# Thirty-six units of the first context pass in rounded products, with the convolution's taps divided anew between GpSimd and VectorE

## The reference, cut to what matters

```python
hc = modulate(rmsnorm(xc, norm1_g[l]), csh1, csc1)      # 256 x 1024
pc = hc @ w_in[l]                                       # 1024 x 4608: 36 tiles of 128 columns
q_c, k_c, v_c = (split_heads(u) for u in jnp.split(pc[..., GLU_END:QKV_END], 3, axis=-1))
...
yc_conv = conv_branch(pc[..., :GLU_END], conv_dw[l], conv_dw_b[l], conv_ln_g[l],
                      conv_ln_b[l], w_conv_out[l])      # 31 taps, 512 channels
yc_attn = merge_heads(context_attention(q_c, k_c, v_c)) @ w_na_out[l]
xc = xc + cg1 * gated_merge(pc[..., QKV_END:], yc_conv, yc_attn, w_out[l])
```

```python
def conv_branch(p_glu, dw, dw_b, ln_g, ln_b, w_o):
    a, g = jnp.split(p_glu, 2, axis=-1)
    u = a * jax.nn.sigmoid(g)
    u = dwconv1d(u, dw, dw_b)
    u = jax.nn.silu(layernorm(u, ln_g, ln_b))
    return u @ w_o
```

## Time and profile before

| what | before |
|---|---|
| times of three executions | 2887.86, 2890.33, 2897.75 us; median 2890.33 us |
| profiled execution | 2888.0 us, span of its instructions 2885.9 us |
| mean granted clock of TensorE | 0.98 of full speed |
| TensorE busy | 2788.7 us, 97% of the span |
| GpSimd, VectorE, ScalarE busy | 1303.7, 1511.6 and 1083.6 us |

### The profile page before, as it was taken

The page is one execution under the profiler, slowest core; times in us unless marked ns, Lnnn a source line. Parts: engine busy times, 40 slices in busy tenths (PEclk is TensorE's granted clock), DMA queues, the critical chain, the costliest instruction groups (busy, mean ns, idle before and its releaser), DMA issues.

```text
span 2885.9 us, 41322 instructions
## 1 busy us (share of the span) xinstructions
PE 2788.7 (97%) x15778; PEld 2293.2 (79%) x15778; DVE 1511.6 (52%) x1960; ACT 1083.6 (38%) x1667; POOL 1303.7 (45%) x752
## 2 busy tenths in 40 slices
PE   8998887999999999999999999999999999999998
PEld 7975744878888878877788888888887778788887
DVE  7855687353323345368874532422454887552535
ACT  4435223333323223235543422322343554342433
POOL 3423323435444264278842322222347884344343
PEclk9989889999999999999999999999999999999999
DMA  5246297323232243432231212121233222232332
GB/s 190 92 169 248 89 276 240 104 94 103 84 106 88 92 128 127 151 99 88 70 93 61 73 59 70 62 66 59 65 104 112 94 66 88 80 102 95 95 102 73
DMA packets 109735, 306.88 MB, mean 106 GB/s; under 512 B 29008, under 2 KB 37328, under 8 KB 109072
## 3 DMA queue, kind: packets, MB, share of 16 engines
q1 hardware_dynamic: 87584, 284.49, 30.7%
q10 hardware_dynamic: 19648, 16.66, 1.9%
q0 software_dynamic: 2352, 3.67, 0.4%
HBM read 294.95 MB, written 7.45 MB: 105 GB/s over the span
## 4 chain that ended last, share of the span: by engine, by line
PE 87%; DVE 5%; issue 2%; POOL 2%; DVEq 1%; ACT 1%; DMA 1%; SPq 0%; ACTq 0%; POOLq 0%
PE ps L296 41%; PE ps L330 17%; PE ps L321 6%; PE ps L1953 3%; PE ps L1949 3%; PE ps L1954 3%; PE ps L1957 3%; PE ps L2366 2%; POOL wlo L257 2%; PE ps L2026 1%; PE ps L2007 1%; PE ps L741 1%; DVE nacc L443 1%; PE ps L1995 1%; PE ps L1997 1%
## 5 line engine op out<-in xcount | busy, mean ns | idle before, releaser
L257 POOL TENSOR_TENSOR wlo<-wraw,whi 128x1024 fp32r<-128x1024 f32 x373 | 923.7, 2487 | 1279.6 <-ACT whi L249 1277.2
L249 ACT ACTIVATE whi<-wraw 128x1024 fp32r<-128x1024 f32 x373 | 391.7, 1055 | 457.6 <-PE ps L296 169.9
L296 PE MATMUL ps<-xah,whi 128*128 128x512 f32 x992 | 387.9, 391 | 1.7 <-issue 1.7
L296 PE MATMUL ps<-xal,whi 128*128 128x512 f32 x992 | 387.4, 391 | 0.0
L296 PE MATMUL ps<-xah,wlo 128*128 128x512 f32 x992 | 280.1, 391 | 0.0
L2252 DVE SCALAR_TENSOR_TENSOR co<-ub,vec,co 128x512 f32<-128x512 f32 (+1 forms) x216 | 255.6, 1222 | 4.2
L296 PEld LDWEIGHTS ps<-xah,whi 128*128 128x128 f32 x992 | 186.1, 188 | 42.7 <-issue 2.7
L296 PEld LDWEIGHTS ps<-xal,whi 128*128 128x128 f32 x992 | 186.1, 188 | 40.3
L296 PEld LDWEIGHTS ps<-xah,wlo 128*128 128x128 f32 x992 | 186.1, 188 | 40.2
L2353 POOL TENSOR_TENSOR co<-co,ct 128x512 f32<-128x512 f32 (+1 forms) x144 | 165.4, 1148 | 20.5
L296 PE MATMUL ps<-hhi,whi 128*128 128x512 f32 x408 | 159.3, 390 | 0.0
(11 more groups left out here) (417 smaller groups left out, 6011.4 us busy)
## 6 DMA issues: line engine op xcount, KB each, us to landing
wraw<-stream SPq DMA_DIRECT2D x425, 512.0 KB, 3.5
wada<-w_ada SPq DMA_DIRECT2D x96, 512.0 KB, 6.7
biasb<-attn_bias ACTq DMA_DIRECT2D x32, 256.0 KB, 3.3
xin<-x0T SPq DMA_DIRECT2D x4, 528.0 KB, 6.4
s_u<-uk ACTq DMA_DIRECT2D x8, 264.0 KB, 2.5
res<-x0T ACTq DMA_DIRECT2D x1, 2048.0 KB, 11.1
outT<-res SPq DMA_DIRECT2D x4, 512.0 KB, 2.6
s_y<-yk POOLq DMA_DIRECT2D x56, 32.0 KB, 5.5
```

What stands on the lines that cost most here:

```text
L249: act.activation(whi[:, s], wraw[:, s], ACT.Copy).then_inc(hi_done[s], 1)
L257: pool.tensor_tensor(wlo[:, s], wraw[:, s], whi[:, s].bitcast(F32), ALU.subtract).then_inc(lo_done[s], 1)
L296: last = pe.matmul(ps[:, bank, 0:b - a], w[:, s, kt], x[:, kt, c0 + a:c0 + b], start=start, stop=stop)
```

## The change

Three things change in pass c0, and the later passes keep their code.

1. Units U to U+35 go the split way (36 units); only U+36 to U+51 stay whole (`N_WHOLE` = 16). So `norm_hi_act` writes `xah` and `norm_scale_dve` also writes `xal` for c0a (eight more VectorE instructions), ScalarE does 36 more `split_hi`, GpSimd 36 more `split_lo`. The `split_hi` of U to U+3 stand in `mlp_act` ahead of the squares m = 4 to 7.
2. GpSimd does taps 0 to 9 of its two tiles (`CTX_TAPS` = 10) and two `split_lo` ahead of each of its nine tap steps; VectorE does the other 21 taps of tiles 0 and 1 behind its own.
3. VectorE does `some(3)` in place of `some(2)` at the end of each stage.

```diff
+CTX_TAPS = 10
-N_WHOLE = 52
-N_UNITS = N_B1 + N_WHOLE + 2 * N_LAYER + 8
-WHOLE = (N_B1, N_B1 + N_WHOLE)
+N_CTX, N_WHOLE = 52, 16
+N_UNITS = N_B1 + N_CTX + 2 * N_LAYER + 8
+WHOLE = (N_B1 + N_CTX - N_WHOLE, N_B1 + N_CTX)
...
     def norm_scale_dve(...):
-            if not one:
-                b = shift(kt) if shift else 0.0
-                dve.scalar_tensor_tensor(ylo[:, kt, 0:T], t(kt), b, yhi[:, kt, 0:T].bitcast(F32),
-                                         ALU.add, ALU.subtract).then_inc(n_lo.sem, 1)
+            b = shift(kt) if shift else 0.0
+            dve.scalar_tensor_tensor(ylo[:, kt, 0:T], t(kt), b, yhi[:, kt, 0:T].bitcast(F32),
+                                     ALU.add, ALU.subtract).then_inc(n_lo.sem, 1)
...
     def mlp_act(act, context):
         for kt in range(NT):
-            norm_hi_act(act, first, kt, CTX, context.modv(0), one=True)
+            norm_hi_act(act, first, kt, CTX, context.modv(0))
         for m in range(NT):
+            if m >= R:
+                split_hi(act, N_B1 + m - R)
             norm_square(act, NORM["final1"], m, lambda kt: res[:, kt], SEQ,
...
     class Pass:
-            self.one = whole(U)
-            self.taps = KTAP if self.one else POOL_TAPS
+            self.one = key == "c0"
+            self.taps = CTX_TAPS if self.one else POOL_TAPS
...
     def pe_filler(pe, p, g):
-        (here if p.one else hi_split)(pe, g, 0, 0)
+        hi_split(pe, g, 0, 0)
...
-        if p.one:
-            for kt in range(NT):
-                last = pe.matmul(o, wraw[:, s, kt], x1[:, kt, 0:p.T], start=kt == 0, stop=kt == NT - 1)
-            last.then_inc(unit_done[s], 1)
-            return
...
     def mix_dve(dve, p):
             if n < p.N:
-                some(1 if p.lat else 2)
+                some(1 if p.lat else 3)
...
     def mix_pool(pool, p):
-        T, l = p.T, p.l
+        T, l, per = p.T, p.l, 2 if p.one else 1
...
         for k in range(1, p.taps):
-            if p.U + 11 + k < p.U + 40:
-                split_lo(pool, p.U + 11 + k)
+            for g in range(p.U + 12 + (k - 1) * per, p.U + 12 + k * per):
+                if g < p.U + 40:
+                    split_lo(pool, g)
...
-        for g in range(p.U + 11 + p.taps, p.U + 40):
+        for g in range(p.U + 12 + (p.taps - 1) * per, p.U + 40):
             split_lo(pool, g)
...
     @block.sync
-            segment(N_B1, N_B1, R)
-            segment(N_B1 + R, N_B1 + R, N_WHOLE - R)
+            segment(N_B1, N_B1, N_CTX - N_WHOLE)
+            segment(WHOLE[0], WHOLE[0], R)
+            segment(WHOLE[0] + R, WHOLE[0] + R, N_WHOLE - R)
...
     @block.gpsimd
-            pool_units(pool, U_GLU, (N_B1 - U_GLU) // R - 1)
+            pool_units(pool, U_GLU, (N_B1 - U_GLU) // R)
```

More of the change, by code:

```diff
@@ L443, in norm_add, with norm_act @@
             dve.tensor_tensor(a, a, nsq[:, kt % 2, 0:T], ALU.add).then_inc(n_acc.sem, 1)
-    def norm_act(act, n, T, eps, split=True, shift=None, dst=None, sums=6, one=False, between=None):
+    def norm_act(act, n, T, eps, split=True, shift=None, dst=None, sums=6, between=None):
         norm_root_act(act, n, T, eps, sums)
@@ L453, in norm_act @@
             for kt in range(NT):
-                norm_hi_act(act, n, kt, T, shift, dst, one)
+                norm_hi_act(act, n, kt, T, shift, dst)
     def root_ahead(act):
@@ L474, in scaled_tile, with norm_hi_act @@
         return ps[:, 4 + kt % 2, 0:T] if n in (NORM["l0a"], NORM["l1a"], NORM["l1b"]) else ntt[:, kt % 2, 0:T]
-    def norm_hi_act(act, n, kt, T, shift=None, dst=None, one=False):
+    def norm_hi_act(act, n, kt, T, shift=None, dst=None):
         act.wait_ge(n_t.sem, n_t.past("t", t_before[n] + kt))
         b = shift(kt) if shift else 0.0
-        act.activation((x1 if one else (dst or halves(T))[0])[:, kt, 0:T], scaled_tile(n, kt, T), ACT.Identity, bias=b).then_inc(n_hi.sem, 1)
+        act.activation((dst or halves(T))[0][:, kt, 0:T], scaled_tile(n, kt, T), ACT.Identity, bias=b).then_inc(n_hi.sem, 1)
     def raw_hi_act(act, n, kt, src, g, dst):
@@ L530, in norm_rows_pe, with norm_dve @@
         last.then_inc(n_row.sem, 1)
-    def norm_dve(dve, n, src, T, gain, split=True, shift=None, dst=None, one=False):
+    def norm_dve(dve, n, src, T, gain, split=True, shift=None, dst=None):
         norm_rec_dve(dve, n, T)
         if split:
-            norm_scale_dve(dve, n, src, T, gain, shift, dst, one)
+            norm_scale_dve(dve, n, src, T, gain, shift, dst)
         else:
@@ L562, in norm_in_place_dve, with norm_scale_dve @@
         dve.drain()
-    def norm_scale_dve(dve, n, src, T, gain, shift=None, dst=None, one=False, also=None):
+    def norm_scale_dve(dve, n, src, T, gain, shift=None, dst=None, also=None):
         r = norm_row_dve(dve, n, T)
@@ L598, in build @@
         done += 0 if "final" in name else NT
-        kept_lo += 0 if "final" in name or name == "c0a" else NT
+        kept_lo += 0 if "final" in name else NT
     g1 = lambda name: (lambda kt: colr(name, 1, kt))
@@ L1755, in mlp_dve @@
             add_unit_dve(dve, N_B1 - 8 + m, 0, 0, m, res, SEQ)
-        norm_scale_dve(dve, first, context.src, CTX, context.gain(0), context.modv(0), one=True)
+        norm_scale_dve(dve, first, context.src, CTX, context.gain(0), context.modv(0))
         for m in range(R, NT):
@@ L1801, in build @@
     shared = {}
-    U_KV = N_B1 + N_WHOLE + N_LAYER
+    U_KV = N_B1 + N_CTX + N_LAYER
     class Pass:
@@ L2030, in whole_of @@
     def whole_of(p, x):
-        return {id(xah): x1, id(hhi): h1, id(mhi): m1}[id(x)] if p.one else x
+        return {id(hhi): h1, id(mhi): m1}[id(x)] if p.one else x
     def mix_pe(pe, p):
-        xh = whole_of(p, xah)
         if p.one:
-            pe_quad(pe, p.U, 0, 0, xh, xal, p.T, between=lambda: norm_sums_pe(pe, NORM["final1"], SEQ), **normed(p.key + "a"))
+            pe_quad(pe, p.U, 0, 0, xah, xal, p.T, between=lambda: norm_sums_pe(pe, NORM["final1"], SEQ), **normed(p.key + "a"))
             norm_rows_pe(pe, NORM["final1"], SEQ)
@@ L2723, in ffn_dve @@
                 add_norm_dve(dve, D, NORM[p.after], p.res, T, gate=p.modv(5))
-    passes = [Pass("c0", 0, False, N_B1), Pass("l0", 0, True, N_B1 + N_WHOLE),
+    passes = [Pass("c0", 0, False, N_B1), Pass("l0", 0, True, N_B1 + N_CTX),
               Pass("c1", 1, False, U_KV), Pass("l1", 1, True, U_KV + 8)]
```

11 lines of the change are left out of this document (5 added, 6 removed).

## The result

| | kernel before | changed kernel |
|---|---|---|
| median of the timed runs | 2890.49 us (2880.12 to 2899.48, 13 runs) | 2904.67 us (2892.64 to 2911.21, 13 runs) |
| ratio to before, 95% interval | | 1.0046 (1.0034 to 1.0058) |
| profiled execution | 2888.0 us, span 2885.9 | 2910.68 us, span 2908.6 |
| VectorE's first row maximum of pass c0 | 1035.05 | 1046.67 |
| `conv_mean_pe`, its first product | 1136.42 | 1154.65 |

Slower, by 14 us at the medians and by 0.46% as a ratio. The profiled execution fits the forecast almost too well (2910.68, the mean at 1154.65 against 1154.5), and a part of that is not the change. The last thing that both kernels do alike ahead of it is the scaling of pass c0's first input tile, line L572. Here it is in three profiles: the kernel before, the changed one, and the changed one once more (count, least/median/most ns, first and last start).

The account below looks back on a forecast made before the run. TensorE, busy 97% of the span, was taken as the bound; the mean 17.9 us later (2 us of the start included) plus 3 us of clock gave 21 us on 2888.0, so 2909 profiled, 2911 median; range 2893 to 2928.

Parts of the forecast that it names:

- no change: Rival, chance 0.14: exclusion holds but stages hide it, only the end pays; mean at 1136.5, total 2887 to 2896 us.
- a split unit: TensorE's term: each of 36 units takes 2.84 us instead of 3.49, saving 23.4 us if nothing else moved.
- The start and the clock: Pass c0's first eight units lose 2 us instead of winning 5; TensorE's lowered clock behind the mean adds 3 us.
- the last turn before 1104: Sign of being wrong: attention stages' last turn before 1104; forecast 1116, before the change 1104.36.
- Into the stages: Before the stages, four of VectorE's eight taps wait for splits, ending 10 us later; first maximum at 1042.
- One stage when VectorE is late: Attention stages: VectorE's 2.0 us plus six taps at 7.8 us make 9.8 us, was 8.75; the first 10.6.
- a stage in which the splits fall on the maximum and the exponentials: Named as what would upset the forecast most: VectorE needs nothing of SBUF's second input there; no size given.
- GpSimd's ring now waits for TensorE: In the attention stages, GpSimd can't run ahead and get out of the way; part of the 9.8 us stage.
- Behind the stages: After the stages VectorE has 52 taps, about 13 beside six splits, 39 alone; mean at 1154.5, 17.9 us later.
- the assumption that a waiting tap gets in between two splits back to back: VectorE's tap gets in as behind single splits; if not, a stage is 0.4 us longer, 3 us in all.
- Faster: Rival, chance 0.11: splits don't hold VectorE for their whole length, taps 0.8 us at most; total 2878 to 2882 us.
- Slower still: Rival, chance 0.17: GpSimd stays saturated, its row about 9 us, clock falls in stages; 10 us more, 2919 to 2930.

Follow-up runs that it names:

- Run 3: Changed kernel with ScalarE's split_hi of U to U+3 one to two squares earlier; ratio to the kernel before 1.0015.
- run 2: Changed kernel with the 21 late taps of tiles 0 and 1 on VectorE left out of the computation; ratio to the kernel before 0.9985.
- run 8: Changed kernel with 29 idle TensorE products between the attention half of U+36 and the mean; ratio to the kernel before 1.0013.
- run 10: Changed kernel with 29 idle TensorE products ahead of the mean, timed once more in another series; ratio to the kernel before 1.0030.
- Run 7: Changed kernel with late taps first in PSUM, four split_hi copies earlier, and two instead of three own taps per tile in a stage; ratio to before 0.9962.
- second series: Changed kernel as it is, timed again in one series with the 29 idle products and both repairs; ratio to the kernel before 1.0039.
- run 5: Changed kernel with VectorE's 42 late taps, summed in PSUM, moved ahead of its own last four taps; ratio to the kernel before 0.9970.
- run 4: Changed kernel with 20 idle TensorE products between the attention half of U+36 and the mean; ratio to the kernel before 1.0040.

## Why the prediction was right, and where its steps were off

Its mechanism and its sign held: TensorE's shorter units are paid for by VectorE's taps, which share their way to SBUF with GpSimd's splits, and the mean comes late. The time, 2904.67, lies 6 us under the 2911 and in the range. That it lies so near is in part luck: the forecast put 17.9 us between the two means, and measured from the anchor there are 6.8 to 8.5. With the anchors laid on each other, on the clock of before, the mean is at 1144.9 in the first profile and at 1143.3 in the second, a little nearer to the 1136.5 of the rival "no change" than to the forecast's 1154.5. Step by step, in the profiled execution and from the anchor:

| step | forecast | measured |
|---|---|---|
| a split unit | 2.84 us | 2.88 (U+30 to U+35) |
| start of c0: the eight units lose | 2 us | 3.7; 2.0 in the second profile |
| first maximum, on the clock of before | 1042 | 1036.9, 1035.2 |
| stages | 10.6, then 9.8 us | 10.66, 9.96, 9.71, then four of 8.34 |
| last turn, on the clock of before | 1116 | 1104.7, 1103.0 |
| last reciprocal to mean | 40.8 us | 42.5 |
| clock behind the mean | 3 us | 3.0 (10.9 against 7.9); 2.5 in the second profile |
| mean later by | 17.9 us | 6.8 to 8.5 |

**The start and the clock** came out as worked. Run 3 confirms the start's cause (ScalarE's copies behind squares that wait for VectorE), runs 2, 8 and 10 the clock's. Of the signs of being wrong, "the last turn before 1104" is met in the second profile and missed by 0.7 us in the first; the terms that made it so early are the next two.

**"Into the stages"** was off by 5 to 7 us. I had GpSimd splitting U+8 to U+15 while VectorE does its first eight taps, with four of them held. One was held (2.6 us), and then GpSimd stood still:

```profile
1040.97 2.48 POOL L257 TENSOR_TENSOR wlo<-wraw,whi 128x1024 fp32r<-128x1024 f32 x1 [0.82 <-ACT whi L249]
1048.79 0.61 POOL L2347 TENSOR_TENSOR ct<-ub,vec 128x256 f32<-128x256 f32 x1 [5.33 <-issue]
```

5.33 us of "issue" ahead of GpSimd's first tap, from 1043.45 on, while VectorE's eight taps ran from 1040.70 in 5.90 us. The kernel before has the same pause (5.32 us), so the row was there to be found; I had read only busy time there.

**"One stage when VectorE is late"** is the mis-sized term. It let both splits of a stage fall on taps (2 x 2.85) and came to 9.8; from the fourth on the measured stage is 8.34, with one tap in six held for 2.5 us. The seven intervals add up to 63.7 us where the forecast had 10.6 + 6 x 9.8 = 69.4. The prediction named this case at its end, "a stage in which the splits fall on the maximum and the exponentials", but gave it no price. The first three intervals are the forecast's stage almost to the tenth. What ended them shows in GpSimd's pairs of splits:

```profile
1051.87 5.11 POOL L257 TENSOR_TENSOR wlo<-wraw,whi 128x1024 fp32r<-128x1024 f32 x2
1060.21 5.07 POOL L257 TENSOR_TENSOR wlo<-wraw,whi 128x1024 fp32r<-128x1024 f32 x2
1068.51 4.85 POOL L257 TENSOR_TENSOR wlo<-wraw,whi 128x1024 fp32r<-128x1024 f32 x2
1076.61 5.09 POOL L257 TENSOR_TENSOR wlo<-wraw,whi 128x1024 fp32r<-128x1024 f32 x2
```

They come every 8.1 to 8.3 us from the start, while VectorE's maxima (1046.67, 1057.33, 1067.29, 1077.00) come every 9.7 to 10.7. So GpSimd, which began 5.2 us behind the first maximum, makes up for its lag and is 0.4 us ahead of the fourth. From then on the first split lies over VectorE's idle 1.1 us and its reads of PSUM, one tap is held in place of two, and VectorE's stage falls to GpSimd's 8.34. So the term rests on one sentence that did not hold, "GpSimd's ring now waits for TensorE, so it can't run ahead and get out of the way": it did, by 5.6 us in three stages. Run 7 shows what the two cost each other: with four taps in a stage the stage is 7.75.

**"Behind the stages"** was right in size (40.8 against 42.5), and the assumption that a waiting tap gets in between two splits back to back held: beside the six splits six taps take 2.4 to 2.6 us each, and the splits 2.52 instead of 2.40.

So two terms of the sum were too large, by 5 to 7 and 5.7 us, and the tail was 1.7 too small: 17.9 - 5.1 - 5.7 + 1.7 = 8.8, against 8.5 in the profiled execution. The forecast's 21 us came nearer to the timed difference than that: the ratio of 1.0046 is 13.3 us, 1.6 to 3.9 more than the traces show up to layer 0, which lies within its interval of 7 us (the second series has 1.0039, 11.3 us).

**The rivals.** "Faster" (splits don't hold VectorE up for their whole length) was to be decided by a tap beside a split under about 1.5 us: they take 2.4 to 2.6, and run 5 shows that it is the second input from SBUF that makes them so. "No change, because the stages hide it" had the mean at 1136.5. Its premise is half true, since the steady stage is shorter than the mean stage of before (8.34 against 8.75) and hides one of the two splits, but the first three stages and the tail are not hidden, and TensorE stands still for 12.4 us. "Slower still" (GpSimd stays saturated) had the row right, for GpSimd doesn't stand still for more than 0.16 us in a steady stage, and the price wrong: its row grows from 8.05 to 8.34 us, not to about 9. The Trainium skill (SBUF — State Buffer, section "SBUF: two separate sides") has the lock exclusive for the first comer's whole instruction. On VectorE's side these runs agree (2.52 us for a tap behind a split). On GpSimd's side they agree only in direction: a pair of splits takes 5.10 us where it takes 4.72 with fewer taps about, and in the tail one tap between two splits costs GpSimd 0.12 us, less than the 0.48 that the tap takes alone.

## What to carry to other kernels

Before moving work to a hidden engine, ask which memory its inputs come from, and whom it meets at the place where the work lands: a tap beside GpSimd's splits costs 0.476 us with its sum in PSUM and 2.4 to 2.6 with it in SBUF. Order them so that what is free of the conflict runs beside GpSimd and the rest when GpSimd is done. The changed kernel had it the other way round and lost 9 to 12 us; with the tail turned round and four copies issued earlier it gains (0.9957 and 0.9975 in two series). Even then it gets 7 to 12 of the 23.4 us that the forecast gave as the most. And compare traces from the last instruction that both do alike, since executions here differed by up to 16.5 us before it (961.8 to 978.3).

## What the hardware showed unexpectedly

- A VectorE instruction with one input in SBUF and one in PSUM and a split of GpSimd don't hold each other up, in either direction: 40 taps at 0.476 us and six splits at 2.40 us at the same time (run 5).
- What two engines that exclude each other cost depends on where they stand to each other. VectorE's stage was 10.66, 9.96 and 9.71 us and then 8.34 four times, without a change in the work: GpSimd's row of 8.1 to 8.3 us slid forward until one of its two splits fell where VectorE reads nothing from SBUF.
- GpSimd stood for 5.3 us without a wait that the profile shows ahead of its first tap of the pass, in both kernels. What it does there is open.
- An idle stretch of 3.7 us of TensorE, behind 8.8 us of idle products, was enough for half clock at the mean (run 4), as were one of 8.9 us (run 7) and one of 12.4 us (the changed kernel); one of 1.3 us (run 5) was not.
